# A hybrid decoder layer on one core: the order of the first loads, and when small vectors are fetched

## What is computed

```python
h = _rmsnorm(x, norm_g[l])
proj = h @ w_in[l]
qa, ka, va, za, qb, kb, vb, zb, fb, qm, zm, gl = _split_cols(proj, IN_WIDTHS)
...
ua = (oa * jax.nn.silu(za)) @ w_proj_a[l]
...
log_f = jax.nn.log_sigmoid(fb.astype(jnp.float32) + b_forget[l].astype(jnp.float32))
ob = _forgetting_attention(qb, kb, vb, log_f).reshape(B, S, B_WIDTH).astype(x.dtype)
ub = (ob * jax.nn.silu(zb)) @ w_proj_b[l]
...
mh = _rmsnorm(mem, mem_norm_g[l])
km, vm = _split_cols(mh @ w_mem_kv[l], (M_WIDTH, M_WIDTH))
...
um = (om * jax.nn.silu(zm)) @ w_proj_m[l]
g = jax.nn.sigmoid(gl.reshape(B, S, N_BRANCH, D_MODEL) + b_gate[l])
merged = g[:, :, 0] * ua + g[:, :, 1] * ub + g[:, :, 2] * um
x = x + (merged @ w_out[l]).astype(x.dtype)
```

## Time and profile before

| what | value |
|---|---|
| median of 3 runs | 1176.38 us (1176.31 to 1177.24) |
| the profiled execution | 1176.61 us |
| its span in the profile | 1174.8 us |
| TensorE busy with matmuls | 1166.8 us |
| VectorE, ScalarE, POOL busy | 727.9, 545.3, 40.6 us |
| granted TensorE clock | 1.00 |

### The profile page before, as it was taken

How to read it: one execution, slowest core, us unless ns; L and a number is a source line. 1 busy time by engine, 2 the same in 40 slices (tenths; PEclk the granted TensorE clock), 3 DMA queues, 4 the chain that set the end, 5 groups by cost and what they waited for, 6 DMA issues and landing times.

```text
span 1174.8 us, 14754 instructions
## 1 busy us (share of the span) xinstructions
PE 1166.8 (99%) x5344; PEld 969.1 (82%) x5344; DVE 727.9 (62%) x897; ACT 545.3 (46%) x670; POOL 40.6 (3%) x31
## 2 busy tenths in 40 slices
PE   8999999999999999999999999999999999999998
PEld 6788888888888888888888888888888888888887
DVE  5868576566576567567576565665556556555653
ACT  5755455444545545545544444434434443443432
POOL 1100000010010000000000000000000000000000
PEclk9999999999999999999999999999999999999999
DMA  9778678568578587687777786577549547765870
GB/s 310 255 244 307 219 235 301 183 212 301 198 251 275 192 268 257 207 263 229 250 249 223 259 259 215 169 225 252 205 145 300 190 154 229 251 202 201 283 244 36
DMA packets 144568, 271.59 MB, mean 231 GB/s; under 512 B 8913, under 2 KB 30085, under 8 KB 144528
## 3 DMA queue, kind: packets, MB, share of 16 engines
q1 hardware_dynamic: 132752, 254.38, 64.8%
q10 hardware_dynamic: 11488, 16.62, 4.4%
q0 software_dynamic: 288, 0.06, 0.1%
HBM read 249.24 MB, written 24.14 MB: 233 GB/s over the span
## 4 chain that ended last, share of the span: by engine, by line
PE 99%; DMA 1%; SPq 0%; DVE 0%; issue 0%
PE acc L1254 32%; PE acc L1256 31%; PE acc L1255 31%; DMA group<-in_x_dram 1%; PE side L1297 1%; PE side L1290 0%; PE side L1313 0%; PE side L1324 0%; PE side L1322 0%; PE side L1320 0%; PE side L1298 0%; PE side L1377 0%; PE side L1345 0%; PE side L1385 0%; PE side L1387 0%; SPq L318 0%
## 5 line engine op out<-in xcount | busy, mean ns | idle before, releaser
L814 DVE TENSOR_TENSOR w_lo<-w_raw,w_hi 128x1024 fp32r<-128x1024 f32 x407 | 496.1, 1222 | 381.1 <-ACT w_hi L504 380.3
L504 ACT ACTIVATE w_hi<-w_raw 128x1024 fp32r<-128x1024 f32 x407 | 430.2, 1060 | 539.5 <-PE acc L1256 534.7
L1254 PE MATMUL acc<-w_hi,hT_hi 128*128 128x512 f32 x1152 | 450.1, 391 | 0.7 <-DVE w_lo L810 0.7
L1256 PE MATMUL acc<-w_hi,hT_lo 128*128 128x512 f32 x1152 | 448.4, 389 | 0.0
L1255 PE MATMUL acc<-w_lo,hT_hi 128*128 128x512 f32 x1152 | 448.3, 389 | 0.0
L1254 PEld LDWEIGHTS acc<-w_hi,hT_hi 128*128 128x128 f32 x1152 | 216.3, 188 | 47.1 <-DVE w_lo L814 1.3
L1256 PEld LDWEIGHTS acc<-w_hi,hT_lo 128*128 128x128 f32 x1152 | 216.2, 188 | 45.1
L1255 PEld LDWEIGHTS acc<-w_lo,hT_hi 128*128 128x128 f32 x1152 | 216.3, 188 | 44.1
L1254 PE MATMUL acc<-w_hi,mT_hi 128*128 128x512 f32 x256 | 100.1, 391 | 0.0
L1255 PE MATMUL acc<-w_lo,mT_hi 128*128 128x512 f32 x256 | 99.6, 389 | 0.0
L1256 PE MATMUL acc<-w_hi,mT_lo 128*128 128x512 f32 x256 | 99.6, 389 | 0.0
(11 more groups left out here) (168 smaller groups left out, 566.0 us busy)
## 6 DMA issues: line engine op xcount, KB each, us to landing
w_raw<-in_w_in_dram SPq DMA_DIRECT2D x142, 1024.0 KB, 5.9
w_raw<-in_w_mem_kv_dram SPq DMA_DIRECT2D x16, 1024.0 KB, 7.4
w_raw<-in_w_out_dram SPq DMA_DIRECT2D x16, 1024.0 KB, 5.2
w_raw<-in_w_proj_a_dram SPq DMA_DIRECT2D x12, 1024.0 KB, 5.1
w_raw<-in_w_proj_m_dram SPq DMA_DIRECT2D x8, 1024.0 KB, 5.0
w_raw<-in_w_proj_b_dram SPq DMA_DIRECT2D x8, 1024.0 KB, 5.1
turned_oz<-group SPq DMA_DIRECT2D x44, 128.0 KB, 4.8
group<-turned_oz SPq DMA_DIRECT2D x11, 512.0 KB, 5.6
```

The source lines that it names most:

```text
L504: act.activation(whi[:, s % RING], raw[:, slot, UK * (s % 2):UK * (s % 2) + UK], ACT.Copy)\
L814: dve.tensor_tensor(wlo[:, s % RING], raw[:, (s // 2) % RING, UK * (s % 2):UK * (s % 2) + UK], whi[:, s % RING].bitcast(F32), ALU.subtract ...
L1254: pe.matmul(banks[t][:], hi, whi[:, s % RING, j], start=first and j == 0, stop=False)
L1256: return pe.matmul(banks[t][:], lo, whi[:, s % RING, j], start=False, stop=last and j == UK - 1)
```

## The change

Weight tile 0 is requested from ScalarE's queue, between x's first piece and mem_norm_g's rows; SP requests tile 1 and only then x's second piece. TensorE turns x's second piece inside unit 0, between the matmuls of its two k-tiles, by a hook `between`, and no longer ahead of unit 0; the stand-in transposes behind x's first piece become eight, where there were six, the turn of the second piece, and six. POOL requests the nine smalls after `xT` has reached 6 (x's fourth piece is turned). The forget columns are requested at ScalarE's unit 5 in place of 1 and split at unit 11 in place of 9, on both engines. The gains' arithmetic on VectorE moves from unit 8 to 12.

```diff
--- before.py
+++ after.py
@@ -95,6 +95,7 @@
 U_SPLIT = (26, 27)
 U_MERGEDT = 4
 U_MERGED_SPLIT = (13, 14)
+U_WF, U_GAINS = (5, 11), 12
 U_LAST_MIX, U_LAST_TURN, L_LAST_TURN, U_LAST_SPLIT = (1, 2), 3, 5, (9, 10)
 OUT_RUNS = ((0, 0, 12), (1, 0, 12), (0, 12, KT), (1, 12, KT), (2, 0, KT), (3, 0, KT))
 OUT_UNITS = [(n, k) for n, k0, k1 in OUT_RUNS for k in range(k0, k1, UK)]
@@ -314,10 +315,8 @@
                             sp.wait_ge(lo_done, u0 + 2 * (last_use(slot, before) - before) + 2)
                         if before is None and i == 0:
 
-                            for j in range(UK):
-                                sp.dma_start(raw[:, 0, j], view[:, j, bass.ds(col, CW)]).then_inc(first_tile_in[j], 16)
-                                if j == 0:
-                                    sp_x(1)
+                            sp.dma_start(raw[:, 0, 1], view[:, 1, bass.ds(col, CW)]).then_inc(first_tile_in[1], 16)
+                            sp_x(1)
                             sp.dma_start(raw[:, 0, UK:], view[:, UK:LK, bass.ds(col, CW)]).then_inc(load_in[0], 16)
                             sp_x(2)
                         elif before is None and i == 1:
@@ -456,6 +455,7 @@
             pool.memset(half[:], -0.5).then_inc(pre["half"], 1)
             pool.wait_ge(pre["half"], 1)
             pool.memset(rel[32:33, :], 1.0).then_inc(pre["rel"], 1)
+            pool.wait_ge(pre["xT"], 6)
             with nc.allow_non_contiguous_dma(reason="vectors of a few hundred words, once"):
                 for i, (g, w) in enumerate(((q_norm_a, 1), (k_norm_a, 1), (q_norm_b, 1), (k_norm_b, 1),
                                             (q_norm_m, 2), (k_norm_m, 2))):
@@ -506,6 +506,8 @@
 
 
             act.dma_start(x_sb[:, :, x_cols(0)], x_v[:, :, x_cols(0)]).then_inc(x_in[0], 16)
+            view, col = body_chunks("m", 0)[0]
+            act.dma_start(raw[:, 0, 0], view[:, 0, col:col + CW]).then_inc(first_tile_in[0], 16)
             act.dma_start(gm_rows, mem_norm_g.rearrange("l (k p) -> (l k) p", p=P)).then_inc(g_in, 16)
 
             act.wait_ge(pre["half"], 1)
@@ -535,7 +537,7 @@
                     act.wait_ge(*(pre["summ"], t) if t else (pre["sumx1"], 3))
                     act.activation(waste, mem_sb[:, t], ACT.Square, accum_out=ssx[:, 2 + t:3 + t])\
                        .then_inc(pre["summ"], 1)
-                if s == 1:
+                if s == U_WF[0]:
 
                     with nc.allow_non_contiguous_dma(reason="eight columns, once"):
                         act.dma_start(wf[:], w_in_v[:, :, F0:F0 + B_HEADS]).then_inc(wf_in, 16)
@@ -548,7 +550,7 @@
                                 o = act.activation(mT[0][:, k], side[j][:, i * S:(i + 1) * S], ACT.Copy,
                                                    scale=gm[:, k:k + 1])
                             o.then_inc(pre["mT_hi"], 1)
-                if s == 9:
+                if s == U_WF[1]:
                     act.wait_ge(wf_in, 16)
                     act.activation(wf_hi, wf[:], ACT.Copy).then_inc(pre["wf_hi"], 1)
                 if s == 17:
@@ -1020,6 +1022,7 @@
                     dve.tensor_scalar(msx[:, 0:2], ssx[:, 0:2], 1.0 / D, EPS, ALU.mult, ALU.add)\
                        .then_inc(pre["meanx"], 1)
 
+                if s == U_GAINS:
                     dve.wait_ge(small_in, 16 * 9)
                     for i in range(AB_GROUPS):
                         c = 0 if i < A_GROUPS else 2
@@ -1255,7 +1258,7 @@
                 pe.matmul(banks[t][:], hi, wlo[:, s % RING, j], start=False, stop=False)
                 return pe.matmul(banks[t][:], lo, whi[:, s % RING, j], start=False, stop=last and j == UK - 1)
 
-            def unit(u0, s, x_pair, k, banks, first, last):
+            def unit(u0, s, x_pair, k, banks, first, last, between=None):
 
                 if not fixed(u0 + s if isinstance(u0, int) else u0, 0):
                     pe.wait_ge(lo_done, u0 + s + 1)
@@ -1266,6 +1269,8 @@
                         pe.wait_ge(pre["x_lo"], k + j + 1)
                     for t in range(TT):
                         o = passes(s, x_pair, k, j, t, banks, first, last)
+                    if between is not None and j == 0:
+                        between()
                 o.then_inc(unit_used, 1)
 
             def chunk_free(c):
@@ -1358,9 +1363,7 @@
             pe.transpose(acc[0][1][:, KT:2 * KT], gm_rows, ident[0:KT, 0:KT]).then_inc(pre["gxT"], 1)
             keep_clock(4)
             tokens_T(0)
-            keep_clock(6)
-            tokens_T(1)
-            keep_clock(6)
+            keep_clock(8)
 
             def beside_first(s):
                 if s in U_X:
@@ -1427,7 +1430,8 @@
                         x_pair = mT
                         if attn is None and s < 2 * CU:
                             pe.wait_ge(pre["mT_lo"], s - CU + 1)
-                    unit(u0, s, x_pair, UK * (s % CU), acc[w % 2], s % CU == 0, s % CU == CU - 1)
+                    unit(u0, s, x_pair, UK * (s % CU), acc[w % 2], s % CU == 0, s % CU == CU - 1,
+                         (lambda: tokens_T(1)) if attn is None and s == 0 else None)
 
             body("m", 0, None)
             body("m", 1, ("m", 0, OZ_M))
```

## The result

The changed kernel takes 1181.13 us (median of 7 runs, 1180.15 to 1181.47), the kernel before 1176.67 beside it (7 runs). The ratio is 1.0035, interval [1.0026, 1.0045]: **slower by 4.5 us** by the medians. The forecast was 1178.3 with 1180.2 as the upper end of its range; "no more than 0.2% from the kernel before" had the largest chance, 0.63.

The account below looks back on a forecast made before the run. TensorE was taken as the bound, busy 1166.8 of 1174.8 us. Head +0.3 and unit 12 +1.6 sum to +1.9 on the median 1176.38: 1178.3 us, its own range 1177.3 to 1179.4, overall range 1176.1 to 1180.2.

Parts of the forecast that it names:

- The two causes: Gain rows delayed behind tile 0 at the start (g, 0.7 us); late side work ahead of mT_lo at unit 12 (+1.6 us).
- g: At the start, delay of the turn of mem's gain rows, requested behind weight tile 0: 0.7 us, between 0.1 and 1.5.
- The credit for quick transposes: Inside g: x's first-piece transposes, coming later, may run faster; up to 0.4 us back, half of that taken.
- rival (c): At the start, a longer TensorE pause leaves the first six matmuls at 1.2 GHz, costing 1.4 us more: 1179.7; chance 0.11.
- The head's other term, -0.44: At the start, unit 2 begins at 16.15 + g against 16.59, so the head is g - 0.44 = +0.3 us.
- The chain that I named: Second piece's hT_hi to the end of unit 1's w_lo: 3.09 us in series, TensorE waiting about 0.9 us.
- Unit 12: Forget columns and gains' arithmetic delay VectorE's mT_lo, so TensorE waits before the forget product: +1.6 us, between 1.2 and 2.0.
- The late requests: Forget columns asked for at unit 5 and small vectors after six turned pairs arrive in time: cost nothing.
- rival (b): Forget columns land late, each us beyond 21.2 of flight stalling unit 12; at 24 us, 1181.1; chance 0.12.
- x's third piece "no longer decides": At the start, x's third piece (landed 12.7 before) comes before 11.6 + g, so it does not set unit 1's start.

Follow-up runs that it names:

- e12: The changed kernel with SP holding back its weight and x requests until both gain rows are in; 1179.46 us.
- e10: The changed kernel with tile 0 requested in two halves of 128 KB and mem's gain rows requested between them; 1180.34 us.
- e6: The changed kernel with fourteen stand-in transposes, not four, ahead of the gain rows' turn; 1180.28 us.
- e1: The changed kernel with mem's gain rows requested ahead of weight tile 0 on ScalarE's queue; 1178.33 us.
- e3: The changed kernel with mem's gain rows requested ahead of tile 0, forget columns split at unit 10 and gains' arithmetic at unit 14; 1176.70 us.
- e2: The changed kernel with forget columns split at unit 10, not 11, and gains' arithmetic at unit 14, not 12; 1179.35 us.
- e4: The kernel before with only the late part: late vector and forget-column requests, columns split at unit 11, gains' arithmetic at unit 12; 1177.27 us.
- e9: The kernel before with late vector and forget-column requests, columns split at unit 10 and gains' arithmetic at unit 14; 1175.73 us.
- e5: e3 with x's second piece turned ahead of unit 0 again, two stand-in transposes between the turns; 1177.20 us.

## Why the prediction was wrong

**The two causes were the two that stood in the forecast; the size of one was wrong.** The term that failed is g, the delay of the gain rows' turn: forecast 0.7 us (bounds 0.1 to 1.5), measured 2.0. Its working had 0.48 for the issue and 0.4 for the tile ahead on the same queue, and e12 fits these roughly: 0.5 and 0.5. What it lacked is the third part, 1.0 us, which comes when the rows stand behind tile 0 while SP's queue moves tile 1 and x's second piece. I had read the 0.4 off two rows of the kernel before that both were asked for ahead of every weight tile, and took it for a place behind one. The two weren't even alike but for the queue: SP's row flew behind the 64 KB identity, ScalarE's behind 256 KB of x. The Trainium skill ("DMA: Bandwidth & Descriptors", section "Issuing engines are not separate DMA queues") says that requests of different engines run on the same 16 DMA engines and interleave; the trace agrees with 4.3 against 3.3 us. I had used that section for its word on the sequencer alone. How the engines share their time, so that half a tile ahead costs as much as a whole one (e10) and SP's traffic costs so much more behind the tile than in front of it, stays open.

**The credit for quick transposes** (0.2 us, inside g) did not come. The quick rate came later together with the work: from the turn to hT_hi it is 2.39 us in both kernels, and the first matmul of unit 0 took 0.74 us for 0.48. This is rival (c) in small. In e6, with the pause filled, the same way takes 1.45 us, so the slow rate was 0.9 us of it in the trace; that it costs as much of the time isn't shown, since e6's 0.85 us is within the noise.

**The head's other term, -0.44, did not come.** With g undone (e1, e3) mT_hi of unit 11 stands at 43.4 to 43.5, as in the kernel before. The chain that I named is real: unit 1 waits 0.94 us for w_lo (forecast 0.9), hT_hi to the end of w_lo is 3.04 us (forecast 3.09). But two steps before it were sized too small. In the changed kernel w_lo of tile 0 is ready at 10.25 and the turn of the second piece starts at 12.03, 1.78 us where I had 1.49; from there to hT_hi (12.73) it is 0.70 where I had 0.55. Together they are 0.44 us, all that the term was to bring. In e3 hT_hi starts at 10.83, not at 10.3.

**Unit 12 was right**: forecast +1.6 us, trace +1.56, by medians 1.8 (e2). The steps are those foretold: wf_lo at 47.14 ahead of mT_lo at 47.35, 2.0 us behind mT_hi, then the gains, then the wait of 1.4 to 1.9 us put down to mT_lo.

**The late requests** held nobody up, as forecast, and rival (b) did not happen: the columns flew 14.4 us, not the 21.2 and more that it needs. That its example came to 1181.1 us, the measured time, is chance. That the late requests would relieve the start I saw and set at nothing, because x's third piece "no longer decides". On the kernel before they are worth 0.9 us (e4, e9), through tile 1 too; in the changed kernel their share was not measured by itself.

Sum by the trace: 1.96 + 1.56 = 3.5 of the span's 3.6 us. By medians the loss is 4.5. The profiled execution (1180.15) was the quickest of its seven; the 0.9 us between falls away with e1 (2.8 in medians against 1.9 in spans), which points at a gain-row landing that varies. It does vary: with the same first requests the turn stands at 6.14 in the changed trace, 6.40 in e2 and 6.61 in e6. There is no trace of a slower execution of the changed kernel itself, so how much of the 0.9 us this explains is open.

## What to carry to other kernels

When a large transfer is moved ahead of a small one on a queue, ask who waits for the small one, and price its flight at its new place, behind the large one and beside the other queues' traffic, not by the flight it had in front. Side work that is moved for the sake of its data must be set against the order of the engine it lands on: small steps put ahead of a step with no slack cost 1.6 us here, with the wait for their own input; one unit earlier and two units later they were free. A stall that a change removes at the start is regained only as far as the serial chain behind the next piece allows.

## What the runs showed of the hardware that I had not expected

48 tiny packets of POOL's queue held 19.1% of the 16 DMA engines for 2 us at a full start; taking the small vectors and the forget columns out of it was worth 0.85 us. Mem's 8 KB of gain rows took 2.8 to 3.1 us ahead of a 256 KB tile on their queue, 4.3 to 4.8 behind it, and 3.3 behind it with SP's queue held back. And TensorE ran unit 0 of e5 at half rate, 0.43 us from matmul to matmul, while the row of granted clock for that stretch (8 to 12 us; us, busy, clock, DMA share, GB/s) reads full speed:

```profile
8.00:12.00 4.00, 4.00 (x12) 1.00 1.01 345
```

The spacing is what tells. The Trainium skill ("TensorE: Matmul & The Clock Gate", section "Wait — 56ns, not 53.3ns?") gives N / 1.2 GHz from start to start at the lower level, 0.427 us for 512 columns, and the trace agrees with 0.43.
